# A trunk of two mixer layers with routed experts on one core: the last projection tile split, two of eight picked by replacement, counts in three products, token rows as the gather's weights

## What is computed

```python
for l in range(DEPTH):                       # DEPTH = 2
    h = rmsnorm(x, g_mix[l])
    merged = ...                             # three mixers, merged by gates
    x = x + merged @ w_out[l]                # [256, 1024] @ [1024, 1024]
    h2 = rmsnorm(x, g_ffn[l])
    y = swiglu(h2, ...) if l % 2 == 0 else moe_ffn(h2, ...)
    x = x + y
return rmsnorm(x, g_final)

def moe_ffn(h, router_w, router_b, w_gate, w_up, w_down):
    logits = h @ router_w + router_b         # [256, 8]
    top_v, top_i = lax.top_k(logits, 2)
    top_p = jax.nn.softmax(top_v, axis=-1)
    gates = jnp.sum(one_hot(top_i, 8) * top_p[..., None], axis=-2)
    y = 0
    for e in range(8):                       # w_gate[e], w_up[e]: 1024 x 3584, w_down[e]: 3584 x 1024
        y = y + gates[..., e:e + 1] * swiglu(h, w_gate[e], w_up[e], w_down[e])
    return y
```

## Time and profile before

| | us |
|---|---|
| median of 3 runs | 1702.33 (1700.69 to 1703.53) |
| profiled execution, its own time | 1701.9 |
| its span | 1700.2 |
| TensorE busy (PE) | 1616.8 (95%) |
| TensorE weight loads (PEld) | 1075.3 (63%) |
| VectorE (DVE) | 487.9 (29%) |
| ScalarE (ACT) | 220.6 (13%) |
| GpSimd (POOL) | 51.1 (3%) |

### The profile page before, as it was taken

One profiled execution on the slowest core, in us unless ns is written; L12 is line 12 of the kernel. 1 busy time (PEld: TensorE's weight loads), 2 busy tenths in 40 slices (PEclk: granted clock), 3 DMA queues, 4 the chain that ended last, 5 costly groups with the idle time before them and its releaser, 6 DMA issues.

```text
span 1700.2 us, 40074 instructions
## 1 busy us (share of the span) xinstructions
PE 1616.8 (95%) x18395; PEld 1075.3 (63%) x18395; DVE 487.9 (29%) x946; ACT 220.6 (13%) x463; POOL 51.1 (3%) x126
## 2 busy tenths in 40 slices
PE   8999999999999999999999998999789997899987
PEld 6888878899998887788834543344333543335433
DVE  1456233576733256524220110101001010010101
ACT  1424111100001326111110000000000000000001
POOL 4000200000000000110000000000000000000000
PEclk9999999999999999999989999999999999999999
DMA  8442225353532532223689999999999999999995
GB/s 237 147 149 100 77 77 180 119 198 132 217 125 67 173 124 100 101 77 122 276 325 380 402 421 424 424 420 426 421 423 424 421 425 422 424 420 410 424 405 246
DMA packets 123329, 462.53 MB, mean 272 GB/s; under 512 B 9932, under 2 KB 20862, under 8 KB 106782
## 3 DMA queue, kind: packets, MB, share of 16 engines
q1 hardware_dynamic: 123166, 459.99, 69.0%
HBM read 458.92 MB, written 1.05 MB: 271 GB/s over the span
## 4 chain that ended last, share of the span: by engine, by line
PE 84%; DMA 10%; SPq 3%; issue 1%; DVE 1%; ACT 1%; DVEq 0%
PE bank L1208 23%; PE bank L459 19%; PE bank L1225 10%; DMA slot<-in_moe_w_down 9%; PE bank L1028 8%; PE bank L1093 4%; SPq L1473 3%; PE bank L983 3%; PE bank L819 2%; PE bank L939 2%; DMA slot<-in_moe_w_gate 1%; PE bank L772 1%; PE bank L1149 1%; PE bank L1159 1%; PE bank L500 1%
## 5 line engine op out<-in xcount | busy, mean ns | idle before, releaser
L1208 PE MATMUL bank<-slot,xg 128*32 128x512 f32 (+1 forms) x5120 | 491.5, 541 | 19.2 <-DMA slot<-in_moe_w_up 10.6
L1208 PEld LDWEIGHTS bank<-slot,xg 128*32 128x32 f32 x5120 | 165.1, 110 | 336.2 <-issue 296.9
L459 PE MATMUL bank<-h,slot 128*128 128x256 f32 x1472 | 331.1, 383 | 3.1 <-issue 3.1
L459 PEld LDWEIGHTS bank<-h,slot 128*128 128x128 f32 x1472 | 277.5, 191 | 46.4 <-issue 10.0
L1225 PE MATMUL bank<-slot,aT 128*32 128x256 f32 x4480 | 249.2, 380 | 30.3 <-DMA slot<-in_moe_w_down 28.5
L1225 PEld LDWEIGHTS bank<-slot,aT 128*32 128x32 f32 x4480 | 144.5, 110 | 134.8 <-DMA slot<-in_moe_w_down 33.9
L2575 DVE TENSOR_TENSOR av<-gs,bank 128x512 f32<-128x512 f32 (+1 forms) x40 | 24.8, 621 | 533.9 <-PE bank L1208 532.7
L1892 ACT ACTIVATE gs<-bank 128x512 f32<-128x512 f32 (+1 forms) x40 | 21.8, 544 | 403.2 <-PE bank L1208 403.2
L983 PE MATMUL bank<-sq,slot 128*128 128x256 f32 x256 | 55.9, 379 | 0.0
L1897 ACT ACTIVATE SpT<-bank 128x512 f32<-128x512 f32 x8 | 4.8, 597 | 388.2 <-PE bank L1238 388.2
L983 PEld LDWEIGHTS bank<-sq,slot 128*128 128x128 f32 x256 | 48.6, 190 | 6.4
(11 more groups left out here) (485 smaller groups left out, 1425.1 us busy)
## 6 DMA issues: line engine op xcount, KB each, us to landing
slot<-in_moe_w_gate SPq DMA_DIRECT2D x32, 2048.0 KB, 22.4
slot<-in_moe_w_up SPq DMA_DIRECT2D x32, 2048.0 KB, 28.0
slot<-in_moe_w_down SPq DMA_DIRECT2D x32, 2048.0 KB, 25.7
slot<-in_moe_w_gate SPq DMA_DIRECT2D x32, 1536.0 KB, 26.1
slot<-in_moe_w_up SPq DMA_DIRECT2D x32, 1536.0 KB, 21.7
slot<-in_moe_w_down SPq DMA_DIRECT2D x32, 1536.0 KB, 22.8
slot<-in_w_in SPq DMA_DIRECT2D x18, 2048.0 KB, 7.9
slot<-in_ffn_w_up SPq DMA_DIRECT2D x5, 2048.0 KB, 7.6
```

The lines of the kernel that those rows point to most:

```text
L459: ins = mm(o, w[:, k, c:c + n], rhs[:, k, :], start=k == 0, stop=k == nk - 1)
L1208: ins = mm(o.rearrange("s (b c) -> s b c", c=32), xg[:, g, k, :], strip(w[:, kk, :], p), start=k == 0, stop=k == KD - 1)
```

## The change

Layer 0 and 1: the last of the four projection tiles becomes two tiles of one block each, with banks, adds and squares of their own (`XPARTS`); the squares are counted by five (`SQ_AT`). The sums of blocks 0 and 1, and in layer 1 the third router group, are issued between the two. The router's products and sums of blocks 6 and 7 are issued block by block, the last transposes behind the sums. SP's sixth expert slot waits for five adds. The mask `sl` comes from `match_replace`, which replaces the first match of each of the eight values it is given; six of them are set to 3e38, which no logit equals. Positions come as count minus 1, or minus 1001 where the expert isn't selected, and the selection matrix is written directly behind them; the gate arithmetic moves behind the first `xg` copies. The counts are three products, two of 16 columns and one of 8. The gather takes 128 x 128 blocks of `ht` as weights and the selection (96 or 64 columns) as the moving side, in two halves of four channel blocks, and the result has channels on partitions; VectorE copies each half (`keep_slots`) where it transposed each group. `gate_bank` waits for two halves instead of each group.

```diff
+XPARTS = ((0, 2), (2, 4), (4, 6), (6, 7), (7, 8))
+SQ_AT = (0, 4, 9, 13)
...
+def logits(ks):
+    for tt in range(NT):
+        for k in ks:
+            mm(tok["rt"][:, tt * NE:(tt + 1) * NE], h[:, k, tt * P:(tt + 1) * P], w_rt[:, k, :],
+               start=tt == 0 and k == 0, stop=False, skip_group_check=True)
+def turn_rows(ks):
+    for tt in range(NT):
+        for k in ks:
+            ins = nc.tensor.transpose(tok[tt][:, k % 4, :], h[:, k, tt * P:(tt + 1) * P], ident[:, :])
+        if ks[-1] % 4 == 3:
+            close_bank(ins, f"ht{tt}{ks[-1] // 4}")
...
-for tt in range(NT):
-    for k in ks:
-        mm(tok["rt"][:, tt * NE:(tt + 1) * NE], h[:, k, tt * P:(tt + 1) * P], w_rt[:, k, :],
-           start=g == 0 and tt == 0 and k == 0, stop=False, skip_group_check=True)
-if g == 3:
-    need(pe, "squares", 4 * ssn + g + 1)
-    close_bank(sums(ks), "rt")
-for tt in range(NT):
-    for k in ks:
-        ins = nc.tensor.transpose(tok[tt][:, k % 4, :], h[:, k, tt * P:(tt + 1) * P], ident[:, :])
-    if g % 2:
-        close_bank(ins, f"ht{tt}{g // 2}")
+logits(ks)
+turn_rows(ks)
...
+if s and g:
+    ins = unit(b[:, 0, :], w, 256, P, sq)
+    close_bank(ins, n)
+    continue
...
-        if l and (s or g) and s + g < 2:
+        if l and (s or g):
             routed(2 * s + g - 1)
-    free_slot(f"{l}wo{s}", f"{l}xo{2 * s + 1}")
+    if s == 0:
+        free_slot(f"{l}wo{s}", f"{l}xo1")
 if l:
     routed(2)
     need(pe, "added", 4)
     sums(range(2))
-    routed(3)
 else:
     b = open_bank(pe, f"st{ssn}")
     need(pe, "added", 2)
     token_sums(b, nsqs[0], range(2), True, False)
-    need(pe, "squares", 4 * ssn + 4)
-    close_bank(token_sums(b, nsqs[0], range(KD - 2, KD), False, True), f"st{ssn}")
+close_bank(unit(v2(open_bank(pe, f"{l}xo4"))[:, 0, :], w, 256 + P, P, sq), f"{l}xo4")
+free_slot(f"{l}wo1", f"{l}xo4")
+for k in (6, 7):
+    if l:
+        need(pe, "xw_ready", k - 2)
+        logits([k])
+    need(pe, "squares", SQ_AT[ssn] + k - 2)
+    if l:
+        ins = sums([k])
+    else:
+        ins = token_sums(b, nsqs[0], [k], False, k == KD - 1)
+close_bank(ins, "rt" if l else f"st{ssn}")
+if l:
+    turn_rows([6])
+    turn_rows([7])
...
-mm(b[:, 0:NE], upto[:, :], sl[:, 0, :], start=True, stop=True)
-mm(b[:, NE:2 * NE], upto[:, :], sl[:, 1, :], start=True, stop=False)
-mm(b[:, NE:2 * NE], ones[:, :], sl[:, 0, :], start=False, stop=True)
-mm(b[:, 2 * NE:3 * NE], ones[:, :], sl[:, 0, :], start=True, stop=False)
-close_bank(mm(b[:, 2 * NE:3 * NE], ones[:, :], sl[:, 1, :], start=False, stop=True), "cn")
+two = b[:, 0:2 * NE].rearrange("p (t e) -> p t e", t=2)
+mm(two, upto[:, :], sl[:, :, :], start=True, stop=False, skip_group_check=True)
+mm(b[:, NE:3 * NE].rearrange("p (t e) -> p t e", t=2), ones[:, :],
+   sl[:, 0:1, :].broadcast_to([P, 2, NE]), start=False, stop=False, skip_group_check=True)
+close_bank(mm(b[:, 2 * NE:3 * NE], ones[:, :], sl[:, 1, :], start=False, stop=True,
+              skip_group_check=True), "cn")
...
-for g in range(ng):
-    for tt in range(NT):
-        for p in range(4):
-            ins = mm(banks[g][32 * p:32 * p + 32, 0:256].rearrange("s (b c) -> s b c", c=32),
-                     Sl[:, tt, 32 * g:32 * g + 32], strip(ht[:, tt, :], p),
-                     start=tt == 0, stop=tt == NT - 1)
+for half in range(2):
+    o = banks[half][:, 0:128 * ng].rearrange("p (k s) -> p k s", k=4)
+    for k in range(4):
+        c = (4 * half + k) * P
+        for tt in range(NT):
+            ins = mm(o[:, k, :], ht[:, tt, c:c + P], Sl[:, tt, 0:32 * ng], start=tt == 0, stop=tt == NT - 1)
...
-pe.wait_ge(S["xg_done"], i * 5 + (NG * s + g + 1))
+if g < 2:
+    pe.wait_ge(S["xg_done"], i * 4 + (2 * s + g + 1))
...
-for g in range(4):
+for g in range(5):
...
-for g in range(4):
+for g, (k0, k1) in enumerate(XPARTS):
     x_part(g)
-    A(dst[:, 2 * g:2 * g + 2, :], x[:, 2 * g:2 * g + 2, :], ACT.Square,
-      scale=1 / 32).then_inc(S["squares"], 1)
+    A(dst[:, k0:k1, :], x[:, k0:k1, :], ACT.Square, scale=1 / 32).then_inc(S["squares"], 1)
...
-for g in range(4):
+for g, (k0, k1) in enumerate(XPARTS):
     b = v2(take(dve, f"{l}xo{g}"))
-    o = x[:, 2 * g:2 * g + 2, :]
-    done(tt_(o, o, b, ALU.add), f"{l}xo{g}")
+    o = x[:, k0:k1, :]
+    done(tt_(o, o, b[:, 0:k1 - k0, :], ALU.add), f"{l}xo{g}")
     if l == 0 and g in (1, 2):
         mix(0, g - 1)
     if l:
         need_sb(dve, f"{l}xo{g}")
-        for k in range(2 * g, 2 * g + 2):
+        for k in range(k0, k1):
             ins = V.tensor_scalar(h[:, k, :], x[:, k, :], col(VA, 24 + k), None, ALU.mult)
-            if k % 2 == 0:
+            if k < k1 - 1:
...
+step(V.memset(mr[:, :, 2:NE], 3e38))
 V.tensor_scalar(nr[:, 0:2], mr[:, :, 0], -1.0, None, ALU.mult).then_inc(S["route"], 1)
-for t in range(NT):
-    step(V.tensor_scalar(sl[:, t, :], lg[:, t, :], mr[:, t, 1:2], None, ALU.is_gt))
-    step(V.tensor_scalar(eqr[:, t, :], lg[:, t, :], mr[:, t, 1:2], None, ALU.is_equal))
-sync()
-step(V.tensor_reduce(out=nr[:, 2:4], in_=sl[:, :, :], op=ALU.add, axis=AX))
-for t in range(NT):
-    step(V.tensor_tensor_scan(csr[:, t, :], eqr[:, t, :], eqr[:, t, :], 0.0, ALU.add, ALU.max))
-sync()
-step(V.tensor_scalar(nr[:, 2:4], nr[:, 2:4], -1.0, 2.0, ALU.mult, ALU.add))
 sync()
 for t in range(NT):
-    step(V.scalar_tensor_tensor(out=eqr[:, t, :], in0=csr[:, t, :], scalar=nr[:, 2 + t:3 + t],
-                                in1=eqr[:, t, :], op0=ALU.is_le, op1=ALU.mult))
+    step(V.match_replace(eqr[:, t, :], mr[:, t, :], lg[:, t, :], -3e38))
 sync()
-tt_(sl[:, :, :], sl[:, :, :], eqr[:, :, :], ALU.add).then_inc(S["route_c"], 1)
+V.tensor_scalar(sl[:, :, :], eqr[:, :, :], -3e38, None, ALU.is_equal).then_inc(S["route_c"], 1)
 need(dve, "route_c", 1)
-need(dve, "route_e", 2)
-step(tt_(gt[:, :, :], sl[:, :, :], ex[:, :, :], ALU.mult))
+step(V.tensor_scalar(csr[:, :, :], sl[:, :, :], 1000.0, -1001.0, ALU.mult, ALU.add))
+def pick(where, ng):
+    for t in range(NT):
+        ins = V.tensor_scalar(Sl[:, t, 0:32 * ng], iota[:, 0:32 * ng], where(t), None, ALU.is_equal)
+    return ins
 sync()
-step(V.tensor_reduce(out=nr[:, 2:4], in_=gt[:, :, :], op=ALU.add, axis=AX))
+b = take(dve, "cn")
+step(tt_(pos[:, :, :], b[:, 0:2 * NE].rearrange("p (t e) -> p t e", t=2), csr[:, :, :], ALU.add))
 sync()
-step(V.reciprocal(nr[:, 2:4], nr[:, 2:4]))
-sync()
-step(tt_(gt[:, :, :], gt[:, :, :], nr[:, 2:4].unsqueeze(2).broadcast_to([P, NT, NE]), ALU.mult))
-b = take(dve, "cn")
-pv = b[:, 0:2 * NE].rearrange("p (t e) -> p t e", t=2)
-step(tt_(pos[:, :, :], pv, sl[:, :, :], ALU.mult))
+pick(lambda t: pos[:, t, 0:1], NG).then_inc(S["sel_item"], 1)
 step(V.scalar_tensor_tensor(out=ekey[:, :], in0=b[:, 2 * NE:3 * NE], scalar=8.0, in1=keyb[:, :],
                             op0=ALU.mult, op1=ALU.add))
 done(V.tensor_copy(tot[:, :], b[:, 2 * NE:3 * NE]), "cn")
 need_sb(dve, "cn")
+V.memset(cst[:, 6:7], 0.0).then_inc(S["av_done"], 3)
 sync()
-step(V.tensor_scalar(pos[:, :, :], pos[:, :, :], 1.0, None, ALU.subtract))
...
-def turn_slots(g):
-    V.transpose(xg[:, g, :, :].rearrange("p k c -> p (k c)"), banks[g][:, 0:256]).then_inc(S["xg_done"], 1)
-for g in range(NG):
-    dve.wait_ge(S["xg_full"], g + 1)
-    turn_slots(g)
+def keep_slots(half, ng):
+    V.tensor_copy(xg[:, 0:ng, 4 * half:4 * half + 4, :],
+                  banks[half][:, 0:128 * ng].rearrange("p (k g c) -> p g k c", k=4, g=ng)
+                  ).then_inc(S["xg_done"], 1)
+for half in range(2):
+    dve.wait_ge(S["xg_full"], half + 1)
+    keep_slots(half, NG)
+need(dve, "route_e", 2)
+step(tt_(gt[:, :, :], sl[:, :, :], ex[:, :, :], ALU.mult))
+sync()
+step(V.tensor_reduce(out=nr[:, 2:4], in_=gt[:, :, :], op=ALU.add, axis=AX))
+sync()
+step(V.reciprocal(nr[:, 2:4], nr[:, 2:4]))
+sync()
+step(tt_(gt[:, :, :], gt[:, :, :], nr[:, 2:4].unsqueeze(2).broadcast_to([P, NT, NE]), ALU.mult))
```

More of the change, by code:

```diff
@@ L1623, in _ @@
                 for g in range(1, 3):
-                    need(gp, "squares", 4 * (2 * l + 1) + g + 1)
+                    need(gp, "squares", SQ_AT[2 * l + 1] + g + 1)
                     if g > 1:
@@ L2599, in item @@
                 if not last:
-                    for g in range(ahead):
-                        dve.wait_ge(S["xg_full"], i * 5 + (NG + 2 * s + g + 1))
-                        turn_slots(g)
+                    for half in range(2):
+                        dve.wait_ge(S["xg_full"], i * 4 + (2 + 2 * s + half + 1))
+                        keep_slots(half, ahead)
             item(0, 0, None)
```

12 lines of the change are left out of this document (3 added, 9 removed).

## The result

The change takes 1705.2 us (median of 20 runs, 1701.31 to 1707.34), the kernel before beside it 1702.35 (20 runs, 1698.28 to 1705.44). The ratio is 1.0015, with a 95% interval of 1.0009 to 1.0022: about 2.6 us slower, less than the 3.4 us that were called tellable, but with this many runs clearly not zero. The forecast was 1701.9, range 1699.3 to 1704.5. **The prediction was wrong**: the time lies above the range.

A forecast was written before the change was run, and what follows sets the result against it. The prediction took the experts' weight stream to bound the kernel, so the first expert item's start counts. +0.45 us (layer 0) and -0.45 (up to the first projection) sum to 0.0 on 1701.9 us; range 1699.3 to 1704.5.

The forecast's parts named there:

- The last projection tile, layer 0: Layer 0's split last tile: sums ahead of the last half tile cost 0.97, halved add and square save 0.52; +0.45 us.
- Layer 1's square root: Layer 1's split last tile: the table load is no longer covered, so the square root comes 0.74 us later.
- The mask: Layer 1's selection: two value loads and replacements bring the mask from 1.87 to 0.81 us, -1.06 us.
- The counts: Layer 1's routing: three products instead of five, two fewer, save 0.86 us, or 0.48 at full clock.
- The copies late next: Before layer 1's first gather: ScalarE's token-row copies end late, so of 1.78 us saved 1.31 is left.
- The gather itself: Layer 1's first gather: 32 weight loads, 23.3 cold and 8.7 at full clock, take 6.05 us.
- The loop: Expert loop: four gathers longer by 2.0 us and three by 1.1, hidden by the weight stream, costing nothing.
- The rule that the end moves with the start of the first item: First expert item: moving its start moves the kernel's end by as much; the stream hides what happens later in the loop.
- the load's price from the Trainium skill: Gather: estimated 107 ns per 128-column load; the gather would take 3.4 us and the sum be 0.4 lower.
- (b): Rival: TensorE's clock stays up; gather -2.6 us, layer 0's dense records -2.3, sum -4.5, 1697.4 us; chance 0.07.
- (c): Rival: TensorE's clock stays down after the new gather, projections start cold; 1705.7 us at 6 us cold; chance 0.04.
- (d): Rival: the loop's longer gathers open a hole in the weight stream, costing 11.3 us, 1713.2 us; chance 0.02.

The follow-up runs named there:

- the doubled gathers: The change with one bank skipped ahead of layer 0's norm-factor spread, with every gather inside the loop issued twice: 1704.31 us, ratio 1.0014 to before.
- the seven products in before: The kernel before with only wide products that nobody reads, five ahead of layer 1's counts and two behind: 1698.1 us, ratio 0.9979.
- the unread products: Wide products nobody reads, in TensorE's idle time: three and four around the counts in the change with the skip, 0.9985; also in layer 0 in the fastest version, 0.9972.
- the change with the skip: The change with one bank skipped ahead of layer 0's norm-factor spread, which then lies in bank 1 instead of bank 0: 1702.82 us, ratio 1.0007 to before.
- the change with the copies first: The change with the skip, and ScalarE's four row copies ahead of its exponentials instead of behind them: 1701.38 us, ratio 0.9993 to before.
- the routing alone: The kernel before with only selection by replacement, three count products, shortened positions and moved gate arithmetic: 1700.19 us, ratio 0.9993.
- the fastest version: Before with new routing, copies first, earlier square-root table load, and unread wide products around layer 1's counts and layer 0's spread: 1697.56 us, ratio 0.9972.

## Why the prediction was wrong

**The step that failed** is in "The last projection tile, layer 0": that the fifth tile costs +0.45 us and nothing else. I costed its instructions and the engines that wait for them, not the bank that it takes from the turn. The list of waits shows it beforehand: `bank_done7` at the norm factor's spread becomes `bank_done0`, in the row above a product that waits for `bank_done0`. The price could be read from the timeline before: eight h products in 3.22 us, the dense layer starting 1.80 us into them, so what waits for their end starts 1.4 us later at least (measured 1.65).

**The rest, by its own steps.**
- Layer 0's sums, add and square: +0.41 measured, +0.45 forecast, right. From the third add to the last it is 0.89 us longer (6.91 to 7.80; forecast 0.97), from there to the square root 2.29 us (2.25).
- Layer 1's square root: +0.61 us from the start of the output projection, +0.74 forecast, and the table load ends last (851.60), behind TensorE's last sums (851.34), as forecast. Right.
- The mask: 1.87 us to 0.69, -1.18 for -1.06. A replacement took 0.15 us and a value load 0.09, and the second load lies beside the first replacement; the forecast had 0.17 and 0.09.
- The counts: 2.34 us to 0.94, -1.40 for -0.86. Too small, as in this execution they ran at full clock (0.37 a pair). Then `Sl` 0.21 behind `pos`, 0.20 forecast.
- The copies late next: right. The gather starts 1.26 us earlier, 1.31 forecast, waiting for `ht`. The half microsecond that the counts gained beyond the forecast went nowhere, for this reason.
- The gather itself: 6.29 us for 6.05, and 6.23 up to the projection where the sum implied 5.86. Both ends were sized well: 7.12 cold for 6.9, 3.78 warm for 3.87. The clock came back as far behind the start as assumed, 5.3 us for 5.0, by these windows of the change:

```profile
860.00:861.00 1.00, 1.00 (x6) 1.00 (x6) 0.52 (x1) 0.00 (x0) 0.00 (x0) 0.50 0.98 418
861.00:862.00 1.00, 1.00 (x7) 1.00 (x6) 0.04 (x1) 0.00 (x0) 0.00 (x0) 0.53 1.07 451
862.00:863.00 1.00, 1.00 (x13) 0.91 (x16) 0.00 (x0) 0.00 (x0) 0.00 (x0) 1.00 0.97 410
```

  Layer 1 as a whole gained nothing (46.07 us to 46.04 from the start of the output projection to the experts' first product), -0.45 forecast.
- The loop: hidden in the main, as forecast; in proportion to the doubled gathers 0.5 us, which the times can't tell from nothing.
- The rule that the end moves with the start of the first item: the seven products in before put that start at 852.87 for 860.58 us (the scatter of the first stretch included), and the rest took 839.83 us for 839.62. No run contradicts it beyond the scatter.
- One step of arithmetic was wrong, without weight for the result. The prediction says that with the load's price from the Trainium skill (TensorE: Matmul & The Clock Gate, LDWEIGHTS) the sum would be 0.4 us lower. That is the difference for a gather at full clock from end to end; with the forecast's own split, 8.7 loads at full clock, it is 0.1. Measured at full clock were 3.78 us, 0.118 a load, near the 3.87 taken from the rows and above the 3.4 that this price gives.

So +1.65 from the bank (at least 1.0 of it behind the dense layer's first group) and about +0.4 from the gather are the 2.1 us that the forecast lacks by its own terms. Of the rest (0.86 at the start, -0.49 and 0.58 in stretches which the change does not touch or touches behind the stream; the -0.49 may hold what the dense layer's first group gave back) single executions can't tell an effect from scatter; the ratio says +2.6 with 1.1 either way. Between 0.5 and 1.2 us stay unassigned.

**The rivals.** (b), the clock stays up, did not come of itself, but its prices were right for the rows: it was forecast at -2.6 for the way to the end of the gather and -2.3 for the dense layer's first records, and the unread products gave -2.6 (46.07 to 43.49, in the change with the skip) and -2.3 (6.04 to 3.73). (c), it stays down for the projections, did not happen in the profiled execution of the change, where the clock was back 1 us before them; it did in that of the change with the copies first. The time landed near the number of (c), 1705.7, while its profile shows another mechanism: no evidence for it. How often the change's other executions have it isn't known. (d) fell above. The slower side had a chance of 0.06, all of it with mechanisms that the trace of before suggested; none was reserved for what a new bank shifts.

## What to carry to other kernels

When an edit opens one buffer more or fewer from a ring, go through the list of waits to the next place that opens a fixed one: a wait that stood there for nothing can become the longest of the path, at no instruction that the edit touches. A stretch of small products costs twice, itself and the clock behind it; a few wide products in idle time that nobody reads may be worth more than shortening the stretch, but if the clock has fallen before they start they hold up what comes behind them. And ask after each saving which engine is late next: here it was the copies, behind them the clock, and for the table load the sums.

## What was unexpected of the hardware

- Wide unread products kept TensorE at its upper level through a stretch of 8-column products and waits in three profiled executions (granted clock 1.00 for 0.80 in 840 to 866 us); in a fourth it fell as they began (0.93).
- With the same code the clock falls at different times: in 850 to 851 us in before, in 847 to 848 with the routing alone, whose list is the same up to there. A stretch behind small products has not one duration but a range: the dense layer's first 32 records took 5.17 to 6.43 us.
- 32 loads of 128x128 with 96 columns behind each take 3.78 us at full clock and 7.12 at half, 0.118 and 0.22 a load; 64 columns change next to nothing (3.68 in the loop, where 96 take 3.71). So the load sets the pace, and the new gather gains nothing from fewer columns.
- ScalarE squares behind a load of the square-root table without another load; the load is 1.28 us and could be moved ahead of the last squares into idle time.
- A replacement of eight values takes 0.15 us at 8 elements, 0.275 at 128.
- One kernel's runs lie up to 9.6 us apart (1694.07 to 1703.68 for the fastest version). Differences under about 1.5 us between kernels could be seen only in the rows, not in the times.
